# A hybrid decoder layer: the norm's row factor applied behind the input projections, a finer first load of x, and a decay chain threaded through the convolutions

## The reference

```
def rms_norm(x, w):
    y = x32 * lax.rsqrt(jnp.mean(x32 * x32, axis=-1, keepdims=True) + RMS_EPS)
    return (y * w).astype(x.dtype)
...
    h = rms_norm(x, norm_w)
    proj = jnp.einsum('btd,de->bte', h, w_in)
...
    qkv = jax.nn.silu(causal_depthwise_conv(gqkv, conv_w))      # gated-delta heads, 4 taps
    g = -jnp.exp(a_log) * jax.nn.softplus(ga + dt_bias)         # their decay, from 12 more columns
    o_gdn = gated_delta_rule(gq, gk, gv, g, beta)
...
    return x + jnp.einsum('bte,ed->btd', y, w_out)
```

## Time and profile before

| | |
|---|---|
| median of 3 runs | 546.07 us (545.38 to 546.70) |
| the profiled execution | 546.18 us, its span in the trace 544.4 us |
| PE busy | 531.1 us, 98% of the span |
| DVE, ACT, POOL busy | 326.8, 276.6, 47.4 us |
| first instruction of PE | 8.42 us after the span's start |
| first product of the projection | 15.64 us |

### The profile page before, as it was taken

One profiled execution on the slowest core, in us unless ns is written; L12 is line 12 of the kernel. 1 busy time (PEld: TensorE's weight loads), 2 busy tenths in 40 slices (PEclk: granted clock), 3 DMA queues, 4 the chain that ended last, 5 costly groups with the idle time before them and its releaser, 6 DMA issues.

```text
span 544.4 us, 8057 instructions
## 1 busy us (share of the span) xinstructions
PE 531.1 (98%) x3116; PEld 444.2 (82%) x3116; DVE 326.8 (60%) x548; ACT 276.6 (51%) x439; POOL 47.4 (9%) x49
## 2 busy tenths in 40 slices
PE   3999999999999999999999999999999999999997
PEld 3887888888888987778888888888888888888885
DVE  2776877768686877546454545466455545646451
ACT  4766564556455553346543554455466446543330
POOL 1003030112031021100100000010010001000000
PEclk9999999999999999999999999999999999999999
DMA  9997664546354643657477656765755665667811
GB/s 277 214 299 178 158 183 124 150 123 157 99 134 125 185 129 106 157 154 183 128 189 193 184 154 183 194 178 154 186 148 157 200 200 178 207 199 227 273 40 40
DMA packets 149930, 91.78 MB, mean 169 GB/s; under 512 B 7843, under 2 KB 139138, under 8 KB 149762
## 3 DMA queue, kind: packets, MB, share of 16 engines
q1 hardware_dynamic: 148562, 88.95, 60.5%
q10 hardware_dynamic: 1328, 2.31, 1.3%
HBM read 89.13 MB, written 2.10 MB: 168 GB/s over the span
## 4 chain that ended last, share of the span: by engine, by line
PE 96%; DMA 1%; ACT 1%; POOL 0%; issue 0%; DVE 0%; ACTq 0%
PE pj L1245 19%; PE pj L1243 19%; PE pj L1246 19%; PE pj L1221 13%; PE pj L1222 6%; PE pj L1287 3%; PE mx L1386 2%; PE mx L1376 2%; PE pj L1292 1%; DMA cst<-table_dram 1%; PE mx L1363 1%; PE pj L1218 1%; PE mx L1277 1%; PE mx L1270 1%; PE pj L1217 1%; PE mx L1460 1%
## 5 line engine op out<-in xcount | busy, mean ns | idle before, releaser
L292 DVE TENSOR_TENSOR w_lo<-w_raw,w_hi 128x1024 fp32r<-128x1024 f32 x160 | 194.5, 1224 | 90.9 <-ACT w_hi L374 90.7
L374 ACT ACTIVATE w_hi<-w_raw 128x1024 fp32r<-128x1024 f32 x160 | 169.1, 1057 | 151.9 <-PE pj L1246 136.6
L1243 PE MATMUL pj<-w_hi,hT 128*128 128x512 f32 x320 | 127.0, 397 | 0.0
L1245 PE MATMUL pj<-w_hi,hT 128*128 128x512 f32 x320 | 126.9, 397 | 0.0
L1246 PE MATMUL pj<-w_lo,hT 128*128 128x512 f32 x320 | 124.9, 390 | 0.0
L1221 PE MATMUL pj<-hT,w_hi 128*128 128x512 f32 x300 | 111.7, 408 | 0.0
L1222 PE MATMUL pj<-hT,w_lo 128*128 128x256 f32 x300 | 84.0, 280 | 0.0
L1245 PEld LDWEIGHTS pj<-w_hi,hT 128*128 128x128 f32 x320 | 60.2, 188 | 12.0
L1246 PEld LDWEIGHTS pj<-w_lo,hT 128*128 128x128 f32 x320 | 60.1, 188 | 12.1
L1243 PEld LDWEIGHTS pj<-w_hi,hT 128*128 128x128 f32 x320 | 60.1, 188 | 12.0
L1221 PEld LDWEIGHTS pj<-hT,w_hi 128*128 128x128 f32 x300 | 56.3, 188 | 12.2
(11 more groups left out here) (220 smaller groups left out, 488.5 us busy)
## 6 DMA issues: line engine op xcount, KB each, us to landing
w_raw<-in_w_in_dram SPq DMA_DIRECT2D x256, 256.0 KB, 3.4
w_raw<-in_w_out_dram SPq DMA_DIRECT2D x64, 256.0 KB, 4.3
big<-in_x_dram SPq DMA_DIRECT2D x8, 256.0 KB, 5.6
out_dram<-sq ACTq DMA_DIRECT2D x8, 256.0 KB, 4.2
big<-in_x_dram SPq DMA_DIRECT2D x1, 1024.0 KB, 5.0
big<-in_x_dram SPq DMA_DIRECT2D x2, 512.0 KB, 7.4
cst<-table_dram SPq DMA_DIRECT2D x1, 682.0 KB, 5.9
cst<-table_dram ACTq DMA_DIRECT2D x1, 196.0 KB, 7.2
```

The lines of the kernel that those rows point to most:

```text
L292: eng.tensor_tensor(w_lo[:, n % NSPLIT, :], w_raw[:, n % NRAW, :], w_hi[:, n % NSPLIT, :].bitcast(F32), ALU.subtract).then_inc(S("lo"), 1)
L374: act.activation(w_hi[:, n % NSPLIT, :], w_raw[:, n % NRAW, :], ACT.Copy).then_inc(S("hi_done"), 1)
L1243: ins = pe.matmul(bank[:, :], src[:, kc, 0, tok], hi[:, k, :], start=first, stop=False)
L1245: pe.matmul(bank[:, :], src[:, kc, 1, tok], hi[:, k, :], start=False, stop=False)
```

## The change

**Norm.** x is no longer scaled. Its raw blocks are transposed and multiplied by the norm's column weights only, the squares are summed in pieces beside the first group, and both row factors are made with one power. PE spreads them over the partitions into `rb` (two transposes). For the gated-delta heads POOL multiplies each result by `rb` after adding its halves, in an instruction of its own. For the other heads ACT's copy to `rows` carries the factor as its scale. The 12 extra columns get it from DVE, in the copy to `abT` that ACT made before.

**Loads.** x comes in five pieces for both halves of the rows, the first two an eighth of its columns each, in between the weight tiles. The identity is loaded first and alone. The small parameters are issued by ACT, in four steps of the first group, and no longer by SP. `keep_busy` transposes 11 times in all and no longer 28. ACT makes the high part of a tile one step of the first group later.

**Order.** The convolutions of group 0 stand between parts of the decay chain on DVE. `LATE` goes from 8 to 16, the first retention and decay units go up as well, `TAP_AFTER` from 6 to 9, and the retention pairs transpose the gated-delta result after their own rows.

```
-U_FIRST = 100
-LATE = 8
-U_RET = {"tail": 1, "tr": 5, "gram": 12, "s1": 16, "o": 24, "out": 48}
+U_CUM = 92
+U_FIRST = 108
+LATE = 16
+U_RET = {"tail": 12, "tr": 6, "gram": 18, "s1": 26, "o": 34, "out": 58}
-TAP_AFTER = 6
+TAP_AFTER = 9
...
+        X_PIECES = [(0, 2), (2, 4), (4, 8), (8, 12), (12, 16)]
...
             for n in range(TILES):
                 load(n)
+                if n in (0, 1, 3, 5):
+                    load_piece(sp, (n + 1) // 2 + 1)
...
-                act.activation(rows[g % 2][:, s].rearrange("p s e -> p (s e)"), pj[2 * (g % 2) + s][:, :], ACT.Copy).then_inc(S("ev_done"), 1)
+                act.activation(rows[g % 2][:, s].rearrange("p s e -> p (s e)"), pj[2 * (g % 2) + s][:, :], ACT.Copy,
+                               scale=sm[:, 6 + s:7 + s]).then_inc(S("ev_done"), 1)
...
-                if b == 0:
-                    scale_first(1)
-                if b < 2:
-                    high_part(b + 1)
+                if b < LEAD:
+                    high_part(b)
                 else:
-                    advance(UPT * (b - 1))
-                if b in (1, 3):
-                    scale_first((b + 3) // 2)
+                    advance(UPT * (b - LEAD + 1))
+                if b % 2:
+                    square_sum(b // 2)
+                if b in (2, 3, 4, 5):
+                    load_params(b - 2)
...
-                pool.tensor_tensor(raw[:, g % 2, s, PAD:], ev[:, n % 2, 0:T], ev[:, n % 2, T:2 * T], ALU.add).then_inc(S("evac"), 1)
+                pool.tensor_tensor(ev[:, n % 2, 0:T], ev[:, n % 2, 0:T], ev[:, n % 2, T:2 * T], ALU.add).then_inc(S("halves"), 1)
+                if n == 0:
+                    pool.wait_ge(S("rb_done"), 1)
+                pool.wait_ge(S("halves"), n + 1)
+                pool.tensor_tensor(raw[:, g % 2, s, PAD:], ev[:, n % 2, 0:T], rb[:, :], ALU.mult).then_inc(S("evac"), 1)
...
+            dve.wait_ge(S("params_psum"), 1)
+            dve.tensor_copy(rb[:, :], mx[3][:, 0:T]).then_inc(S("rb_done"), 1)
+            dve.tensor_copy(pcol[:, KC:], mx[2][:, KC:R_ROWS]).then_inc(S("param_cols"), 1)
+            dve.wait_ge(S("rb_done"), 1)
+            dve.wait_ge(S("abt_psum"), 1)
+            dve.tensor_tensor(abT.rearrange("p (a t) -> p a t", a=2), mx[0][0:32, :].rearrange("p (a t) -> p a t", a=2),
+                              rb[0:32, :].unsqueeze(1).broadcast_to([32, 2, T]), ALU.mult).then_inc(S("abt_done"), 1)
             advance(66)
...
-            for sec in range(3):
-                conv(0, 0, sec)
...
             dve.tensor_tensor(ab[:, A_T1], ab[:, A_Z], ab[:, A_T1], ALU.min).then_inc(S("negabs_z"), 1)
+            conv(0, 0, 0)
             dve.wait_ge(S("exp_z"), 1)
...
             link(dve.tensor_tensor(ab[:, A_T2], ab[:, A_T2], ab[:, A_T3], ALU.mult))
+            conv(0, 0, 1)
             dve.wait_ge(S("ln_u"), 1)
...
+            conv(0, 0, 2)
             advance(90)
...
-            keep_busy(14)
-            pe.wait_ge(S("x0_scaled"), 1)
+            keep_busy(3)
             for b in range(2):
-                x_blocks(b, 0)
-            keep_busy(6)
-            pe.wait_ge(S("x1_scaled"), 1)
-            for b in range(2):
-                x_blocks(b, 1).then_inc(S("hT_psum"), 1)
-            keep_busy(8)
+                pe.wait_ge(S(f"x_in{b}"), 16 * C)
+                for c in range(C):
+                    ins = x_blocks(b, c)
+                ins.then_inc(S("hT_psum"), 1)
+                keep_busy(4)
...
+            pe.wait_ge(S("rstd_done"), 1)
+            for c in range(C):
+                pe.transpose(mx[3][:, c * P:(c + 1) * P], sm[:, 6 + c:7 + c].broadcast_to([P, P]), ident)
             pe.wait_ge(S("param_in"), 5 * 16)
...
-            stream(88)
+            stream(U_CUM)
```

More of the change, by code:

```diff
@@ L297, in x_again, with load_piece @@
             return big[:, (n % 4) * 512:(n % 4 + 1) * 512]
+        X_PIECES = [(0, 2), (2, 4), (4, 8), (8, 12), (12, 16)]
+        def load_piece(eng, i):
+            piece = slice(X_PIECES[i][0] * P, X_PIECES[i][1] * P)
+            for c in range(C):
+                eng.dma_start(x_sb[:, c, piece], x[0, c * P:(c + 1) * P, piece]).then_inc(S(f"x_in{i}"), 16)
         block = ctx.enter_context(nc.Block())
@@ L303, in _ @@
         def _(sp):
[L304 to L307, removed]
+            load_piece(sp, 0)
             def load(n):
@@ L366, in _ @@
         def _(act):
-            act.dma_start(prow[R_NORM:R_CONV, :], norm_w[0].rearrange("(k p) -> k p", p=P)).then_inc(S("norm_in"), 16)
-            act.dma_start(cst[:, 0:K_FIRST], table[:, 0:K_FIRST]).then_inc(S("cst_in"), 16)
+            act.dma_start(cst[:, 0:P], table[:, 0:P]).then_inc(S("ident_in"), 16)
+            act.dma_start(prow[R_NORM:R_CONV, :], norm_w[0].rearrange("(k p) -> k p", p=P)).then_inc(S("ident_in"), 16)
+            act.wait_ge(S("pad_zero"), 1)
+            act.activation(sm[:, 44:45], raw[:, 0, 0, 0:1], ACT.Copy)
+            act.dma_start(cst[:, P:K_FIRST], table[:, P:K_FIRST]).then_inc(S("cst_in"), 16)
             def high_part(n):
@@ L431, in advance, with square_sum, load_params @@
                 pos[0] = max(pos[0], u)
[L434 to L454, removed]
+            def square_sum(i):
+                if i:
+                    act.wait_ge(S("ss_act"), i)
+                act.activation(junk_a[:, 0:4 * P], x_sb[:, 0, i * 4 * P:(i + 1) * 4 * P], ACT.Square,
+                               accum_out=sm[:, i:i + 1]).then_inc(S("ss_act"), 1)
+            def load_params(i):
+                if i == 0:
+                    act.dma_start(wab[:, :, :], w_in[0, :, AB_COL:AB_COL + AB].rearrange("(k p) c -> p k c", p=P)).then_inc(S("wab_in"), 16)
+                elif i == 1:
+                    act.dma_start(prow[R_CONV:R_RET, :], conv_w[0].rearrange("j (t c) -> (j t) c", c=P)).then_inc(S("param_in"), 16)
+                elif i == 2:
+                    act.dma_start(prow[R_RET:R_GDN, :], ret_norm_w[0]).then_inc(S("param_in"), 16)
+                    act.dma_start(prow[R_GDN:R_Q, :], gdn_norm_w).then_inc(S("param_in"), 16)
+                else:
+                    act.dma_start(prow[R_Q:R_K, :], q_norm_w).then_inc(S("param_in"), 16)
+                    act.dma_start(prow[R_K:R_ROWS, :], k_norm_w).then_inc(S("param_in"), 16)
+            act.wait_ge(S("norm_cols"), 1)
             for b in range(KC // 2):
-                act.wait_ge(S("norm_cols"), 1)
                 act.wait_ge(S("hT_psum"), b + 1)
@@ L624, in mix_ret @@
                 gate_tanh(p)
+                if PAIRS[p - 1][0] == "gdn":
+                    advance(U["tail"] + 2)
+                split_last_gdn(p)
                 advance(U["s1"] + 1)
@@ L694, in _ @@
             pool.wait_ge(S("cst_in"), 16)
-            for c in range(C):
-                pool.wait_ge(S("ms_done"), c + 1)
-                power(6 + c, 10 + c, 1).then_inc(S("rstd_done"), 1)
+            pool.wait_ge(S("ss2"), 2)
+            power(6, 10, 2).then_inc(S("rstd_done"), 1)
             def split_y(p, y0):
@@ L885, in _ @@
             dve.wait_ge(S("tanh_b"), 1)
-            dve.tensor_scalar(ab[:, A_BETA], ab[:, A_TB], 0.5, 0.5, ALU.mult, ALU.add).then_inc(S("beta_done"), 1)
+            dve.tensor_scalar(ab[:, A_BETA], ab[:, A_TB], 0.5, 0.5, ALU.mult, ALU.add)
+            conv(0, 0, 2)
             advance(90)
```

75 lines of the change are left out of this document (29 added, 46 removed).

## The result

The changed kernel is slower: 548.68 us median (546.94 to 549.73, 13 runs) against 546.10 (545.38 to 546.76, 13 runs), ratio 1.0041 with the 95% interval [1.0031, 1.0052]. The prediction said 542.2 and gave slower 0.11. The profiled execution took 549.24 us.

The account below looks back on a forecast made before the run. PE, busy 531.1 of 544.4 us, was taken as the bound. Terms -6.3 and +2.4 gave -3.9 us on 546.18, so 542.3, or 542.2 for the median; range 538.8 to 545.2, the forecast's own 541.2 to 543.6.

Parts of the forecast that it names:

- Term 2: Behind the first group: abT wait removed, PE waits 2.7 us for tile 11's low part; +2.4 us, bounds -0.4 to +5.3.
- Term 1: At the start: first useful product moves from 15.64 to 9.0, less 0.3 for the array's pace; -6.3 us.
- The first product: At the start on PE: first useful product near 9.0 us, or the start was sized wrongly.
- the fourth rival: First group: array stays at low pace, each half-pace step costing 3.24 us; 548.4 with two; chance 0.10.
- The tanh: On ACT behind the first group: tanh (L488) done some 13.7 us after the seventh step begins, after waits for POOL.
- No stall from the parameter loads on ACT: First group: a rival said parameter loads stall ACT and PE waits about 1.7 us; 543.9; chance 0.13.
- none from the identity: At the start: a rival said the identity lands late, at 7.95, making term 1 -2.7; 545.8; chance 0.12.
- both rivals: First group and start: parameter loads stall ACT (543.9, chance 0.13); identity lands late (545.8, chance 0.12).
- No wait after 60 us: Sign on PE: no wait between 60 and the output projection.
- The rest, at nothing: After the first group: POOL's doubled additions, later units and ACT's scale cost 0, hidden by ACT's lead.
- the cover: Mixing of the pairs: ACT's high parts 8.4 us ahead hide POOL's work; without it, up to 22 us lost.

Follow-up runs that it names:

- e1: The changed kernel with 26 useless identity transposes on PE just before tile 11, in place of its wait: 545.41 us, ratio 0.9997.
- e3: The kernel before, with four useless DVE products ahead of the low parts of tiles 11 to 13, so that PE pauses: 552.68 us, ratio 1.0114.
- e4: The changed kernel with 11 products of zeros ahead of everything and five more fill-in transposes between x's first two pieces: 548.72 us, ratio 1.0048.
- e8: e7 with e4's warm start: 543.87 us, ratio 0.9959.
- e6: The changed kernel without POOL's product by the row factor for the first pair's two heads: 543.61 us, ratio 0.9971.
- e12: e7 with LATE back at 8 and the old retention units 1, 5, 12, 16, 24, 48: 548.64 us, ratio 1.0047.
- e7: e2 with the low part of tile 16 also made ahead of the decay's clipping: 543.86 us, ratio 0.9964.
- e10: e7 with the decay's column sums behind unit 98, first decay rows behind unit 110, and e4's warm start: 544.04 us, ratio 0.9963.
- e2: The changed kernel with tile 11's low part ahead of the decay chain, and those of tiles 12 and 13 ahead of the last convolution: 544.28 us, ratio 0.9965.
- e5: The changed kernel with group 0's three convolutions put back ahead of the decay chain on DVE: 547.98 us, ratio 1.0021.

## Why the prediction was wrong

**The step that failed** is the price of Term 2: "PE stands 2.7 us at tile 11 ... its first instruction after the wait being ... 2.3 us later", +2.4 and nothing behind it. The mechanism, the place and the size were right (3.1 for 2.7). But the pause was priced as a pause, where e1, e3 and the windows show that it costs 2.8 to 3.4 us more at half the clock. I cited the rule for the start alone and wrote that "no row here shows the second" half, that idling loses the clock; it belonged to my own forecast, which had a pause of 2.7 us in it. With it the sum was −0.5, about no change.

**Term 1, mis-sized.** The first product at 9.33 for 9.0 was near, by two errors that cancel in part: the identity and the norm's weights were there at 3.78 and not 4.3, and PE stood 1.1 us for piece 1, which the text had landed at 5.7 and never waited for (it landed at 7.71). The slow pace was taken as 0.3 us and was 2.0: I let the pace change 5 us after PE's first work, at 9.5, as the fill-in transposes of before had it, and it came about at the end of the first step. e4 shows that it is the array's pace. The 2.0 are those of this one profile; the others with the same start lost 0.7 to 2.0. So the fourth rival happened by half (0.6 of a step, where it decides from 1.3), and the forecast's own pause did the rest. Together: −0.5 + 0.3 + 1.7 = +1.5.

**Left out.** The power, 0.6 us of waiting, and 0.2 more for `rb`'s transposes: nothing in the text asks what stands between the last sum of squares (done at 34.7) and `rb`'s transposes. (In the profiles of e4 to e8 the power took 0.70 us and PE didn't wait for it.) The wait itself was 0.4 larger. Sum: −3.9 + 3.4 + 0.3 + 1.7 + 0.6 + 0.2 + 0.4 = +2.7, where the traces stand 2.6 apart behind the low clock.

**Right for a wrong reason.** The tanh was forecast 13.7 us after the seventh step and stood at 13.1. I had it wait for POOL. ACT did wait for POOL at the third and fourth evacuation (1.38 and 0.82 us), but its taps were done at 43.3, and by its row the tanh waited 0.49 more for PE's product. And what held the chain's first step (44.37) was no longer the tanh but DVE's own two low parts, done at 44.4. The DVE block behind it was 1.6 longer than forecast, and PE came to tile 11 1.0 later (20.2 us from the seventh step and not 19.2). Near hits of several errors gave a wait near the right size. e6 shows that POOL's second instruction does make the block late: without it the block takes 1.3 us less.

**The rest.** No stall from the parameter loads on ACT, and none from the identity, landed with the norm's weights by 3.78: both rivals fell. No wait after 60 us, as said. "The rest, at nothing" held for the change but not as argued: I put the cover at 8.4 us of ACT's lead everywhere, and e12 shows that, with the low parts moved as in e7, the later units are what covers the first pair.

**Still open.** Which pauses cost the clock. In the profiled runs 3.1, 3.4, 3.6, 3.8 and 5.5 us did, 1.8 in e6 did, and 1.2 in e7 and 2.5 in e8 did (3.4 us of low clock), while 1.9 in e10 and 1.2 in e2 did not. Nor is it shown why the change's own 13 runs spread: those at a mean clock of 0.996 or 0.997 took 546.94 to 547.59, the others, 0.989 to 0.993, 547.9 to 549.73.

## What to carry to other kernels

Where a forecast puts a pause of microseconds into an engine that is 98% busy, ask what the engine does after it: here 3.1 us of waiting cost 6.5, and filling it with useless transposes won 3.3 back. Time saved at the start is kept only if the whole chain behind it moves too; follow the transfers on its queue, since a table that nobody needs yet took 1.8 us back. An instruction added to an idle engine isn't free if its neighbour reads the same memory: look for rows of that engine that last as long as the neighbour's.

## What the runs showed of the hardware

- Around a pause of PE the granted clock goes to the lower level for 6.8 to 6.9 us (the change, e3, e6, e12) or 3.4 to 3.5 (e4, e5, e7, e8). It fell between 1.3 us before PE's return (e3) and 1.4 us after it (e6), and costs half of the part in which PE works.
- In the first step of the change the clock column reads 1.00 while products take 3.76 us for eight, 2.08 in the next step. The column isn't to be trusted at a kernel's start; the durations are.
- POOL's operations wait out DVE's low parts: 3.05 us for a POOL addition beside two low parts, 4.13 for a product beside three (e7, the row below), 0.74 alone. DVE's convolutions are held up in turn, 2.01 us beside a POOL product for 1.52. What an overlap costs changes between executions: the power took 1.80 us in the change and 0.70 in e7, with the low part 0.03 us behind it in both.

```profile
40.39 4.13 POOL L728 TENSOR_TENSOR raw<-ev,rb 128x256 f32<-128x256 f32 x1
```
